# Hybrid encoder step: page clears spread over the merge, value differences on VectorE, later query block, earlier copy

## What is computed

```python
z = einsum('bqhd,bkhd->bhqk', q, k) * SB_DIM ** -0.5         # branch A, 8 heads x 64
log_1mb = where(mask, log_sigmoid(-z), 0.0)
after = cumsum(log_1mb, axis=3, reverse=True) - log_1mb
att = where(mask, exp(log_sigmoid(z) + after), 0.0)
o_sb = einsum('bhqk,bkhd->bqhd', att, v)
# branch B: gated linear attention (GLA); branch C: softmax attention into 256 memory tokens
p = einsum('btnc,ncd->btnd', stack(o_sb, o_gla, o_mem), w_branch)
h = x + sum(sigmoid(gates) * p, axis=2) @ w_out              # the merge
h = h + experts(rmsnorm(h))                                  # top 2 of 8 experts in the top group of 4
```

## Time and profile before

| | |
|---|---|
| runs shown, us | 1847.64, 1847.95, 1852.86; median 1847.95 |
| the profiled execution, us | 1844.7, of which the span from first to last instruction is 1843.1 |
| busy share of the span | TensorE 95%, its weight loads 85%, VectorE 57%, ScalarE 47%, GpSimd 7% |
| granted TensorE clock, mean | 0.98 of full speed |
| moved from and to memory | 286.08 MB read, 39.87 MB written |

### The profile page before, as it was taken

How to read it: one execution, slowest core, us unless ns; L and a number is a source line. 1 busy time by engine, 2 the same in 40 slices (tenths; PEclk the granted TensorE clock), 3 DMA queues, 4 the chain that set the end, 5 groups by cost and what they waited for, 6 DMA issues and landing times. The chain is left out here.

```text
span 1843.1 us, 25654 instructions
## 1 busy us (share of the span) xinstructions
PE 1758.2 (95%) x10354; PEld 1560.5 (85%) x10354; DVE 1048.9 (57%) x1275; ACT 866.6 (47%) x1122; POOL 120.9 (7%) x138
## 2 busy tenths in 40 slices
PE   9998999999999999999999999989999999999980
PEld 7887887989898899999999988878888888888870
DVE  5326665443254431232334155568889998898967
ACT  4224554322453331121122133257878878788753
POOL 0022000000000030000000000010001000000003
PEclk9999999999999999999999999989999999999995
DMA  5241110102022263111112142179999999999958
GB/s 188 81 113 34 30 31 23 49 24 73 24 67 75 58 179 99 41 48 40 52 46 86 30 178 88 56 278 396 418 415 416 411 415 417 413 413 415 413 225 302
DMA packets 139321, 329.85 MB, mean 179 GB/s; under 512 B 13674, under 2 KB 91334, under 8 KB 114501
## 3 DMA queue, kind: packets, MB, share of 16 engines
q1 hardware_dynamic: 123556, 272.69, 40.0%
q0 software_dynamic: 10896, 38.74, 5.7%
q10 hardware_dynamic: 4752, 16.78, 2.2%
HBM read 286.08 MB, written 39.87 MB: 177 GB/s over the span
## 5 line engine op out<-in xcount | busy, mean ns | idle before, releaser
L2492 DVE TENSOR_TENSOR low<-raw,hig 128x2048 fp32r<-128x2048 f32 x192 | 431.6, 2286 | 57.4 <-ACT hig L2227 57.0
L2227 ACT ACTIVATE hig<-raw 128x2048 fp32r<-128x2048 f32 x192 | 359.5, 1916 | 22.1 <-ACT ye L2300 14.4
L2055 PE MATMUL bank<-hig,xel 128*128 128x512 f32 x512 | 202.5, 396 | 0.5 <-DVE xel L2563 0.5
L2057 PE MATMUL bank<-hig,xeh 128*128 128x512 f32 x512 | 199.9, 390 | 0.0
L2056 PE MATMUL bank<-low,xeh 128*128 128x512 f32 x512 | 199.3, 389 | 0.0
L70 PE MATMUL bank<-xhi,glo 128*128 128x384 f32 (+1 forms) x552 | 180.8, 328 | 3.8 <-ACT sg L2161 2.3
L72 PE MATMUL bank<-xhi,ghi 128*128 128x384 f32 (+1 forms) x552 | 180.6, 327 | 0.0
L71 PE MATMUL bank<-xlo,ghi 128*128 128x384 f32 (+1 forms) x552 | 180.6, 327 | 0.0
L70 PE MATMUL gproj<-xhi,glo 128*128 128x384 f32 (+1 forms) x384 | 130.2, 339 | 1.0 <-ACT qr L1255 1.0
L72 PE MATMUL gproj<-xhi,ghi 128*128 128x384 f32 (+1 forms) x384 | 125.4, 326 | 0.0
L71 PE MATMUL gproj<-xlo,ghi 128*128 128x384 f32 (+1 forms) x384 | 125.2, 326 | 0.0
(11 more groups left out here) (425 smaller groups left out, 3515.1 us busy)
## 6 DMA issues: line engine op xcount, KB each, us to landing
raw<-in_w_e_gate_dram SPq DMA_DIRECT2D x64, 1024.0 KB, 7.9
raw<-in_w_e_up_dram SPq DMA_DIRECT2D x64, 1024.0 KB, 8.3
raw<-in_w_e_down_dram SPq DMA_DIRECT2D x64, 1024.0 KB, 7.5
graw<-in_w_in_dram SPq DMA_DIRECT2D x39, 512.0 KB, 3.8
expert_rows<-ye ACTq DMA_DIRECT2D x31, 512.0 KB, 8.1
xt<-in_x_prompt_dram SPq DMA_DIRECT2D x16, 512.0 KB, 3.6
expert_rows<-nil POOLq DMA_DIRECT2D x16, 512.0 KB, 10.3
braw<-in_w_branch_dram SPq DMA_DIRECT2D x24, 256.0 KB, 2.8
```

The source lines that it names most:

```text
L2055: nc.tensor.matmul(bank[:, :], xel[n % 2][:, kk, :], wh[:, k, :], start=(kk == 0), stop=False)
L2057: last = nc.tensor.matmul(bank[:, :], xeh[n % 2][:, kk, :], wh[:, k, :], start=False, stop=(kk == KC - 1))
L2227: nc.scalar.activation(hig[q % HI][:, :], raw[q % RAW][:, :], ACT.Copy).then_inc(high, 1)
L2492: nc.vector.tensor_tensor(low[q % RAW][:, :], raw[q % RAW][:, :], hig[q % HI][:, :].bitcast(F32), ALU.subtract).then_inc(lowed, 1)
```

## The change

- The value differences of blocks 0 to 7 move from GpSimd to VectorE: 0 to 3 before the low half of query block 0 (`q_low(0, 0)`), 4 behind it, 5 to 7 in round 1. GpSimd keeps block 8 (now counted by its own semaphore, `lastdiffed`) ahead of the cache differences. In round 1 each `average` waits only for the differences that it reads.
- Query block `(0, 1)` and its high and low halves move from round 0 to round 1, behind the long scores; `q_split(1)` moves from round 1 to round 2.
- In stage 2 ScalarE drains unit 2, with the weight split that follows it, before `grow(0)`.
- In stage 3 clear b waits until part b has ended; the loop on GpSimd becomes sixteen issues.

The values computed are the same.

```diff
--- before.py
+++ after.py
@@ -217,8 +217,8 @@
             ctx, "q", "wq_in ck_in cv_in qwh qwl qprod ckturned pahigh palow glrd qbuilt")
         scored, sdone, scanned, tfilled, tcopied, used, ocopied, overlaid = sems(
             ctx, "sb", "scored sdone scanned tfilled tcopied used ocopied overlaid")
-        early_in, late_in, last_in, vcol_in, vdiffed, cvdiffed, vlast = sems(
-            ctx, "vd", "early_in late_in last_in vcol_in vdiffed cvdiffed vlast")
+        early_in, late_in, last_in, vcol_in, vdiffed, lastdiffed, cvdiffed, vlast, vzeroed = sems(
+            ctx, "vd", "early_in late_in last_in vcol_in vdiffed lastdiffed cvdiffed vlast vzeroed")
         block = ctx.enter_context(nc.Block())
         kout = io["out2"].rearrange("l b t h d -> (l b t) (h d)")
         vout = io["out3"].rearrange("l b t h d -> (l b t) (h d)")
@@ -323,10 +323,6 @@
             pool.drain()
             pool.sem_inc(const, 1)
 
-            def differ(j):
-                r = rows_of(j)
-                nc.gpsimd.tensor_tensor(vn[0:r, j, :], shifted(j)[0:r, :], vn[0:r, j, :], ALU.subtract).then_inc(vdiffed, 1)
-
             def cache_differ(hp):
                 pool.wait_ge(cv_in, 64 * hp + 64)
                 nc.gpsimd.tensor_tensor(cvs[:, :, :], cvsh[:, :, :], cvs[:, :, :], ALU.subtract).then_inc(cvdiffed, 1)
@@ -339,27 +335,20 @@
             last.then_inc(qbuilt, 1)
             pool.wait_ge(kcopied, NT)
             pool.drain()
-            nc.gpsimd.memset(vsh[0][0:1, 0, :], 0.0)
+            nc.gpsimd.memset(vsh[0][0:1, 0, :], 0.0).then_inc(vzeroed, 1)
             pool.wait_ge(vprod, NT)
             nc.gpsimd.memset(over[:, 0:T - DEC - P], 0.0)
+            nc.gpsimd.memset(cvsh[0:1, 0, :], 0.0)
             pool.drain()
             nc.gpsimd.affine_select(out=over[:, T - DEC - P:T - DEC], in_=ones[:, :], compare_op=ALU.is_ge, fill=0.0,
                                     base=0, pattern=[[1, P]], channel_multiplier=-1)
             pool.drain()
             pool.sem_inc(overlaid, 1)
-            pool.wait_ge(vstored, 16 * FULL)
-            pool.wait_ge(early_in, 48)
-            pool.wait_ge(late_in, 48)
-            for j in range(FULL):
-                differ(j)
-            pool.wait_ge(vcopied, NT)
-            nc.gpsimd.memset(cvsh[0:1, 0, :], 0.0)
-            pool.drain()
-            cache_differ(0)
             pool.wait_ge(vlast, 16)
             pool.wait_ge(last_in, 48)
-            differ(FULL)
-            for hp in range(1, HW):
+            nc.gpsimd.tensor_tensor(vn[0:DEC, FULL, :], shifted(FULL)[0:DEC, :], vn[0:DEC, FULL, :],
+                                    ALU.subtract).then_inc(lastdiffed, 1)
+            for hp in range(HW):
                 cache_differ(hp)
 
         @block.tensor
@@ -487,7 +476,9 @@
                 if x == "d" and i == 0:
                     pe.wait_ge(cvdiffed, hp + 1)
                 if t == 0 and i == 1:
-                    pe.wait_ge(vdiffed, NT)
+                    pe.wait_ge(lastdiffed, 1)
+                if t == 1:
+                    pe.wait_ge(vdiffed, 2 * i + 2)
                 for j in range(2 * i, min(2 * i + 2, x + 1)) if x != "d" else (range(4) if i == 0 else [4]):
                     for u in range(2):
                         U = slice(64 * u, 64 * u + 64)
@@ -539,7 +530,7 @@
                     score(t)
                 for f in F[:2]:
                     average(t - LAG, f)
-                if t == 0:
+                if t == 1:
                     query(0, 1)
                 for f in F[2:]:
                     turn(t - LAG, f)
@@ -600,7 +591,7 @@
                 act.wait_ge(qprod, 3 * b + place_in_block(b, g) + 1)
                 if b < HW:
                     if b == 1:
-                        act.wait_ge(vdiffed, NT)
+                        act.wait_ge(vdiffed, FULL)
                     last = nc.scalar.activation(qh[b % 2][:, c0:c0 + n], PQ[:, 0:n], ACT.Copy, scale=SBD ** -0.5)
                     if g == 2:
                         if b:
@@ -679,7 +670,7 @@
                     q_high(hp + 1, QSTEP[hp].index(i))
                 if t < NR and i == CSTEP and hp + 1 < HW:
                     c_high(hp + 1)
-                if t == 1:
+                if t == 2:
                     q_split(1)
                 if t < NR and i == SSTEP and hp + 2 <= HW + 1:
                     q_split(hp + 2)
@@ -716,6 +707,15 @@
                 ve.wait_ge(vprod, t + 1)
                 src = half(tb, t % 2)
                 nc.vector.tensor_copy(vn[0:rows_of(t), t, :], src if t < FULL else src[P - DEC:P, :]).then_inc(vcopied, 1)
+
+            def differ(j):
+                if j == 0:
+                    ve.wait_ge(vzeroed, 1)
+                    ve.wait_ge(vstored, 16 * FULL)
+                    ve.wait_ge(early_in, 48)
+                elif j == 2:
+                    ve.wait_ge(late_in, 48)
+                nc.vector.tensor_tensor(vn[:, j, :], shifted(j), vn[:, j, :], ALU.subtract).then_inc(vdiffed, 1)
 
             def k_low(t):
                 r = rows_of(t)
@@ -796,7 +796,10 @@
                 k_low(t)
                 if t + 2 == NT:
                     q_split(0)
+            for j in range(4):
+                differ(j)
             q_low(0, 0)
+            differ(4)
             for t in range(NR + LAG + 1):
                 hp, i = t // NP, t % NP
                 if t > LAG and len(fill[t - LAG - 1]) > 2:
@@ -805,13 +808,15 @@
                     collect(t - LAG)
                 for n in unit[t] if t < NR else []:
                     scan(n)
-                if t == 0:
+                if t == 1:
                     q_low(0, 1)
+                    for j in range(5, FULL):
+                        differ(j)
                 if t < NR and i in QSTEP[hp]:
                     q_low(hp + 1, QSTEP[hp].index(i))
                 if t < NR and i == CSTEP and hp + 1 < HW:
                     c_low(hp + 1)
-                if t == 1:
+                if t == 2:
                     q_split(1)
                 if t < NR and i == SSTEP and hp + 2 <= HW + 1:
                     q_split(hp + 2)
@@ -1366,9 +1371,9 @@
             w_high(1)
             take([0])
             softplus(0)
-            take([1])
+            take([1, 2])
             grow(0)
-            take(range(2, 8))
+            take(range(3, 8))
             take([8])
             softplus(1)
             take(range(9, 13))
@@ -1850,8 +1855,9 @@
                            io["b_fine"][0, :, :].rearrange("g e -> (g e)").partition_broadcast(P)).then_inc(router_in, 16)
             nc.gpsimd.memset(nil[:, :], 0.0)
             pool.drain()
-            with pool.Fori(0, OVER) as b:
-                dst = ysd[bass.ds(b * P + NE * P, P), :].rearrange("p (a c) -> p a c", c=256)
+            for b in range(OVER):
+                pool.wait_ge(branched, 3 * b + 3)
+                dst = ysd[b * P + NE * P:b * P + NE * P + P, :].rearrange("p (a c) -> p a c", c=256)
                 pool.dma_start(dst, nil[:, :].unsqueeze(1).to_broadcast([P, D // 256, 256])).then_inc(cleared, 16)
             pool.wait_ge(cleared, 16 * OVER)
             pool.wait_ge(merged, 3 * STEPS)
```

## The result

The changed kernel takes 1834.99 us, median of 6 runs (1832.39 to 1837.34), against 1847.5 of the kernel before (6 runs): ratio 0.993, 95% interval 0.9918 to 0.9942. That is 12.5 us by the medians; 11.8 were forecast (1836.1). In a later session it came out at 0.9932 (0.9918 to 0.9945). The forecast held, and most of its steps did. Two things behind the sum did not: what the projection order is worth, and where TensorE's clock falls. (A fall is here a stretch in which the granted clock is 0.50; the gated stage is stage 2.)

A forecast was written before the change was run, and what follows sets the result against it. TensorE, busy 95% of the span, was taken as the bound, so only its waits and low clock could pay. Terms 6.8 + 1.0 + 4.0 = 11.8 us, taken from 1847.95, gave 1836.1 us, range 1830 to 1843.

The forecast's parts named there:

- Attention, 6.8 us: Attention stage: long-score transposes 5.9 us earlier, 0.9 given back, 1.8 from no clock fall; 6.8 us, range 4.5 to 7.7.
- wait on the copy that was to be late next: Attention, following round: ScalarE's split starts at 141.8 on late query weights, holding the first long-score copy to 143.4; 0.9 us lost.
- Cover, differences 0 to 3: Attention, VectorE: these four differences end at 129.35, hidden before work starting at 130.51, with 1.1 us to spare.
- the 0.4 us of the rule on shared interfaces: Attention: if GpSimd still subtracts at 134.4, long scans end 1.6 us later and the gain shrinks 0.4 us; left out.
- The value column: Attention: its load lands about with the query weights, costed at nothing; the next wait if over 1 us behind them.
- Gated, 1.0 us: Gated-attention stage: unit 2's copy and split fit ScalarE's idle time, removing TensorE's wait; 1.0 us, range 0.5 to 1.1.
- What follows (router, experts) starts from TensorE's progress and shifts whole: After the edited stages: later work moves earlier by the full 11.8 us, giving 1832.9 for the profiled execution.
- Merge, 4.0 us: Merge stage: spreading sixteen clears removes a 2.35 us late start and 1.6 us of low clock; 4.0 us, range 0 to 4.5.
- clears holding back each load (1866): Rival, merge: each clear delays a branch load, losing 1.6 us in each of 16 steps, 26 us; 1866, chance 0.03.
- late rows (1843): Rival, attention: late shifted rows hold VectorE and eat the stage's gain; 1843; chance 0.08, shared with two rivals together.
- the burst is not what held the gate load: Rival, merge: spreading the clears gains nothing there; 7.8 us in all, 1840.1, chance 0.08.
- the low clock stays in the attention stage: Rival, attention: remaining gaps or light work lower the clock anyway; 4.5 instead of 6.8 us, 1838.4; chance 0.17 with late loads.

The follow-up runs named there:

- the filled waits: The kernel before, with TensorE filling its two round 0 waits on GpSimd with 17 and 14 transposes of unused output: 1846.31 us, ratio 0.999.
- Moving the split: The changed kernel with ScalarE's weight split behind the two copies of the long scores instead of ahead of them: 1833.43 us, ratio 0.9918.

## Why the prediction was right

**Attention, 6.8 us: right, and for its reasons.** The averages came at 138.96 (near 139 said), the transposes of the long scores at 139.83 (140.1), no fall from 130 to 150. That the fall goes with the waits is the best supported step: none of the seven profiles with the whole attention part has time at 0.50 between 120 and 170, and all seven without it have 3.4 to 10.2 us. (It is not the standing on GpSimd alone that brings it: the differences alone and the filled waits had it too.) The wait on the copy that was to be late next came where it was put, at 1.4 us in one profile and 1.1 in the other for the 0.9 forecast: the split started at 142.14 instead of 141.8 and its two copies followed. In the profiled pair the gated stage starts 6.27 us sooner. That execution of before had a short fall; the three other profiles of kernels with both GpSimd waits start the stage at 320.1 on the mean (clears alone, projection order alone, both), 7.0 us behind the mean of the changed kernel's two (313.16). Moving the split showed the wait on the copy to be ScalarE's order.

**Cover, differences 0 to 3.** VectorE after, beside the earlier trace rows:

```profile
126.37 1.37 DVE L718 TENSOR_TENSOR vn<-vsh,vn 128x512 f32<-128x512 f32 x2
127.90 1.29 DVE L718 TENSOR_TENSOR vn<-vsh,vn 128x512 f32<-128x512 f32 x2 [0.16 <-DMA vsh<-vn]
130.51 0.56 DVE L734 SCALAR_TENSOR_TENSOR ql<-mixed,qh 128x384 fp32r<-128x384 f32 x1 [1.32 <-ACT qh L595]
130.99 0.68 DVE L718 TENSOR_TENSOR vn<-vsh,vn 128x512 f32<-128x512 f32 x1
131.67 2.42 DVE L753 TENSOR_TENSOR_SCAN sfx<-sfx 128x576 f32<-128x576 f32 x1
134.48 4.47 DVE L758 TENSOR_TENSOR_SCAN sfx<-sfx,over 128x1024 f32<-128x1024 f32 x2 [0.40 <-ACT sfx L622]
```

They end at 129.19 with 1.32 us to spare (129.35 and 1.1 said). GpSimd's subtractions ran at 129.57 and 131.59 and were over when the long scans began, so leaving out the 0.4 us of the rule on shared interfaces was right: 4.47 us, the undisturbed 4.46 of the earlier trace rows. The first scan took 2.42 us instead of 1.36 beside GpSimd's cache difference, which the prediction has nowhere, but the long scans still waited 0.40 us for ScalarE, so it cost nothing. The value column was costed at nothing, and a wait on it was named as a sign of being wrong: VectorE stood 1.24 us on it at 142.44. Nothing came of it on TensorE, since the weights were as late; that the two fell together is luck.

**Gated, 1.0 us: the step that failed.** The wait was read off one row, and that row was of an execution in which the clock had fallen just ahead (327 to 331): TensorE reached the copy about 1.6 us late and found the rest of the wait. The clock of before in that stretch, and its wait:

```profile
327.00:331.00 4.00, 4.00 (x15) 4.00 (x15) 1.96 (x3) 2.72 (x3) 0.00 (x0) 0.57 0.01 2
...
340.80 0.41 PE L70 MATMUL gproj<-xhi,glo 128*128 128x384 f32 x1 [1.03 <-ACT qr L1255]
```

The same product with the clears alone, where no fall stands ahead of it:

```profile
341.57 0.41 PE L70 MATMUL gproj<-xhi,glo 128*128 128x384 f32 x1 [2.64 <-ACT qr L1255]
```

In all six other profiles with the old order it is 2.6 us. Taken alone, the new order saves that and, in the profiles, the fall of 3.4 us as well (4.6 us by medians; 339.3 to 334.84 in the stage). In the changed kernel more falls take its place, so that the stage lost 2.5 us in the profiled pair. Term mis-sized: 1.0 for 2.6. Assumption that failed: "What follows (router, experts) starts from TensorE's progress and shifts whole" held for the instructions and their waits, but for 0.5 us at the step into the merge stage, and not for the clock.

**Merge, 4.0 us: right for the profiled execution.** From the first product of the stage to the first of its fifth gate projection TensorE took 81.4 us before and 77.2 in all eight profiles without the burst, 4.2 less. The second of these products before and after:

```profile
738.86 0.34 PE L70 MATMUL bank<-xhi,glo 128*128 128x384 f32 x1
...
730.87 0.34 PE L70 MATMUL bank<-xhi,glo 128*128 128x384 f32 x1
```

As worked out: the wait of 2.3 us, and 1.7 for the fall. In the other profiles with the burst the wait was 1.0 to 2.2 us. The fall is not certain, though: with the burst it came in two of six profiles (before, and projection order alone), so the step is worth some 2.3 us typically (1.8 for the mean of the six waits, and a third of 1.7). The clears alone measured 3.7 by ratio (1.7 to 5.9), which holds both that and the 4.0. That the execution read had the fall is luck for this term.

**Sum.** 11.8 forecast, 12.5 measured, with more from attention and the projection order and less kept in the gated stage than the terms say. The closeness is in part luck: attention alone measured 8.7 us by ratio for its 6.8, the order alone 4.6 for its 1.0, and the falls in the gated stage, which no term has and which cost 5.1 and 3.4 us in its two profiles, took much of the excess back. **The rivals**: clears holding back each load (1866) and late rows (1843) did not show; "the burst is not what held the gate load" fell with the clears alone; "the low clock stays in the attention stage" was wrong about the place and right that low clock is not simply removed. Ahead of 1250 us both profiled kernels spend 23.9 us at 0.50, but the second profile of the changed kernel has 17.1, the attention part alone 10.2, and the six of other kernels without the whole attention part 17.1 to 27.3. Over all runs the mean granted clock rose from 0.979 (74 runs) to 0.982 (12 runs), so some is saved on average: 0.003 of 1840 us is 5.5 us, an upper bound, as part of the low clock fell on waits.

## What to carry to other kernels

The length of a wait in one profile is what is left of it after whatever else made the engine late; before taking it as the gain, look at the clock in the stretch ahead and at a second execution. When two things hold the same place (an engine's backlog and the order of TensorE's own work), measured one at a time they give 3.2 and 0 us up to the next stage, together 6.3 to 7.0. A long run of DMA issues that nobody needs soon should be spread over the loop. With runs of four the worst gate load was 6.2 us, as with single ones; one timed run is too little to say that they cost the same. And a load whose consumer stands in order ahead of more urgent copies is better taken behind them.

## What the runs showed of the hardware

- The granted clock went to 0.50 for 3.4 to 10.2 us at a time, and work in such a stretch took up to twice as long (eight transposes 1.97 us instead of 1.09). One began in the middle of unbroken work (346, with TensorE busy without a gap since 320), and the same kernel had falls at 346 and 448 in one execution, at 320 and 348 in another.
- VectorE's scan of 576 columns in place took 1.36 us in the kernel before, beside GpSimd's value differences, and 2.42 after, beside its cache difference, which itself took 1.29. GpSimd's same 128x512 subtraction took 2.97 us at 145.15 and 1.29 at 237.96, each time beside a pair of 896-column scans that took 5.0 us. The Trainium skill, GPSIMD Engine Reference, section Key points, speaks of shared interfaces and of contention with VectorE instructions that have two SBUF inputs. All these scans have two; the 2.42 and the 2.97 us agree, the 1.36 and the 1.29 at 237.96 show that not every such meeting costs.
